# The choice of experts spread over more weight halves, its softmax moved into the expert stage, and the last norm run among the product segments

## The reference

```
sc    = einsum('nhcd,hckd->nhck', q, sub_keys)       # 8 heads, 2 sides, 128 keys
s_top, i_top = top_k(sc, 16)
cand_s = s_top[:,:,0,:,None] + s_top[:,:,1,None,:]   # 16 x 16 sums of a head
best_s, pos = top_k(cand_s, 16)                      # 16 experts of a head
g     = softmax(best_s)
a     = gelu(hc . u[expert]) * g                     # u, v: 16384 x 1024
out   = sum over experts of a * v[expert]
...
h = h + sigmoid(rmsnorm(h) @ w_gate) * e             # last unit of the last layer
return rmsnorm(h, final_norm)
```

## Time and profile before

| | us |
|---|---|
| median of 3 runs (lowest, highest) | 2161.31 (2157.17, 2176.56) |
| the profiled execution, its span | 2159.17, 2157.3 |
| PE, DVE, ACT busy | 1987.1 (92%), 1481.0 (69%), 1207.8 (56%) |
| first expert stage, of it the choice | 380 to 747, 382 to 579 |
| mean granted TensorE clock | 0.957 |

### The profile page before, as it was taken

How to read it: one execution, slowest core, us unless ns; L and a number is a source line. 1 busy time by engine, 2 the same in 40 slices (tenths; PEclk the granted TensorE clock), 3 DMA queues, 4 the chain that set the end, 5 groups by cost and what they waited for, 6 DMA issues and landing times. The chain is left out here.

```text
span 2157.3 us, 43967 instructions
## 1 busy us (share of the span) xinstructions
PE 1987.1 (92%) x15940; PEld 1904.1 (88%) x15940; DVE 1481.0 (69%) x3043; ACT 1207.8 (56%) x2367; POOL 0.2 (0%) x4
## 2 busy tenths in 40 slices
PE   6998888999999898999999896897999988899996
PEld 6887888999999866999999896897999987799996
DVE  5667655999845499666666587764787567468855
ACT  4455654777765588555555557102565553666544
POOL 0000000000000000000000000000000000000000
PEclk9999998999999999999999997986999989899998
DMA  5433334455566500565656461001565533156552
GB/s 188 147 98 108 121 114 127 150 180 177 177 196 192 174 0 0 185 194 193 191 193 192 136 188 57 1 1 34 179 192 177 185 110 102 36 171 195 177 177 68
DMA packets 96223, 295.98 MB, mean 137 GB/s; under 512 B 9315, under 2 KB 25830, under 8 KB 95974
## 3 DMA queue, kind: packets, MB, share of 16 engines
q1 hardware_dynamic: 96102, 294.35, 43.2%
HBM read 293.26 MB, written 1.05 MB: 136 GB/s over the span
## 5 line engine op out<-in xcount | busy, mean ns | idle before, releaser
L423 DVE TENSOR_TENSOR w_low<-ring,w_high 128x512 fp32r<-128x512 f32 x1102 | 747.9, 688 | 385.3 <-ACT w_high L417 378.0
L449 PE MATMUL bank<-a_high,w_high 128*128 128x256 f32 x3256 | 933.1, 287 | 78.7 <-DVE w_low L423 36.8
L450 PE MATMUL bank<-a_low,w_high 128*128 128x256 f32 x3256 | 916.0, 281 | 0.0
L451 PE MATMUL bank<-a_high,w_low 128*128 128x256 f32 x3256 | 915.6, 281 | 0.0
L417 ACT ACTIVATE w_high<-ring 128x512 fp32r<-128x512 f32 x1102 | 676.6, 627 | 394.2 <-PE bank L451 389.9
L449 PEld LDWEIGHTS bank<-a_high,w_high 128*128 128x128 f32 x3256 | 622.5, 191 | 94.8 <-issue 44.8
L450 PEld LDWEIGHTS bank<-a_low,w_high 128*128 128x128 f32 x3256 | 623.8, 192 | 0.7
L451 PEld LDWEIGHTS bank<-a_high,w_low 128*128 128x128 f32 x3256 | 623.9, 192 | 0.0
L449 PE MATMUL bank<-s_high,w_high 128*128 128x256 f32 x1024 | 283.4, 277 | 2.0 <-DVE s_low L2215 2.0
L450 PE MATMUL bank<-s_low,w_high 128*128 128x256 f32 x1024 | 283.4, 277 | 0.0
L451 PE MATMUL bank<-s_high,w_low 128*128 128x256 f32 x1024 | 283.4, 277 | 0.0
(11 more groups left out here) (351 smaller groups left out, 2041.4 us busy)
## 6 DMA issues: line engine op xcount, KB each, us to landing
ring<-in_stream SPq DMA_DIRECT2D x279, 512.0 KB, 3.6
ring<-in_peer_u SPq DMA_DIRECT2D x128, 512.0 KB, 3.5
ring<-in_peer_v SPq DMA_DIRECT2D x128, 512.0 KB, 3.5
ring<-in_stream SPq DMA_DIRECT2D x32, 256.0 KB, 3.2
x<-in_x SPq DMA_DIRECT2D x4, 256.0 KB, 5.5
arena<-in_mem SPq DMA_DIRECT2D x1, 1024.0 KB, 11.8
out<-x SPq DMA_DIRECT2D x4, 256.0 KB, 2.6
consts<-in_consts SPq DMA_DIRECT2D x1, 640.0 KB, 8.6
```

Source lines behind the costliest of these rows:

```text
L423: self.nc.vector.tensor_tensor(self.w_low[:, h % SLOTS, :], self.raw(h), self.w_high[:, h % SLOTS, :].bitcast(F32), ALU.subtract)\
L449: self.nc.tensor.matmul(to, lh, rh, start=start, stop=False, **more)
L450: self.nc.tensor.matmul(to, lh, rl, start=False, stop=False, **more)
L451: return self.nc.tensor.matmul(to, ll, rh, start=False, stop=stop, **more)
```

## The change

Three edits. (1) In the choice, `best` calls `low()` after every second operation instead of every third for the 128-column tiles, and five times in seven operations instead of every second for the 256-column ones. The choice's scratch starts at column block 96 instead of 84, `hit` moves into `hn`, and ScalarE's first loop has 24 turns instead of 20. (2) The softmax leaves its own block: VectorE subtracts the maximum right after the choice, ScalarE does its three copies and the exponential after turn 24, VectorE normalises after its turn 26, TensorE transposes before its last turn into banks 4 and 5, and VectorE copies the turned numbers at its end. (3) `finish` becomes `last_norm`, a segment whose squares and gains are duties with the keys of the additions to x.

```
-        scratch = 84 * T
+        scratch = 96 * T
-        free_from = 80 // RING
+        free_from = 96 // RING
... TensorE
-                with pe.Fori(1, turns) as it:
+                with pe.Fori(1, turns - 1) as it:
                     turn(it)
+                pe.wait_ge(weighed.sem, weighed.at(1))
+                for n in range(3):
+                    for t in range(TT):
+                        at = (n % 2) * T + t * P
+                        ins = nc.tensor.transpose(self.bank[4 + n // 2][:, at:at + P],
+                                                  side[:, n, t, :], self.const("ident"))
+                ins.then_inc(spun.up(), 1)
+                turn(turns - 1)
... ScalarE
                 act.wait_ge(chosen.sem, chosen.at(1))
-                with act.Fori(free_from, turns) as it:
+                turn(free_from)
+                act.wait_ge(shifted.sem, shifted.at(1))
+                nc.scalar.activation(number, side[:, 0:2, :, :], ACT.Copy)
+                nc.scalar.activation(one, self.const("ident"), ACT.Copy)
+                nc.scalar.activation(less, self.const("iota"), ACT.Copy, scale=-1.0)
+                nc.scalar.activation(g, g, ACT.Exp).then_inc(expd.up(), 1)
+                with act.Fori(free_from + 1, turns) as it:
                     turn(it)
... VectorE
-                with dve.Fori(whole, turns) as it:
+                link(nc.vector.tensor_copy(total.unsqueeze(2), g[:, :, 0:1]))
+                nc.vector.tensor_tensor(g, g, ..., ALU.subtract).then_inc(shifted.up(), 1)
+                for it in range(whole, free_from + 3):
+                    for h in range(it * halves, (it + 1) * halves):
+                        self.split_low(dve, first + AHEAD + h)
+                dve.wait_ge(expd.sem, expd.at(1))
+                link(nc.vector.tensor_reduce(total, g, AX, ALU.add))
+                link(nc.vector.reciprocal(total, total))
+                nc.vector.tensor_tensor(g, g, ..., ALU.mult).then_inc(weighed.up(), 1)
+                with dve.Fori(free_from + 3, turns) as it:
                     for h in range(halves):
                         self.split_low(dve, first + AHEAD + h, it, halves)
+                dve.wait_ge(spun.sem, spun.at(1))
+                for n in range(3):
+                    nc.vector.tensor_copy(turned[:, n, :],
+                                          self.bank[4 + n // 2][:, (n % 2) * T:(n % 2 + 1) * T])
... choose_experts
-        hit = self.at(at + 1024 + 8 * T, PH * PK, PK)
+        hit = self.hn[:, :, :].rearrange("p c (n r) -> p (c n) r", r=PK)
-                done[0] += 1
-                if done[0] % every == 0:
+                done[0] += some
+                if done[0] >= of:
+                    done[0] -= of
                     low()
-            best([... for i in range(r, r + 4)], 3)
+            best([... for i in range(r, r + 4)], 1, 2)
-                best([... for i in range(h, h + 4)], 2)
+                best([... for i in range(h, h + 4)], 5, 7)
... last_norm(self, before, name), in place of finish
+        got, keys = before.ready(name)
+        for c in range(0, DC, 2):
+            duties += [(keys[c], 6, "square", c), (keys[c], 7, "gain", c)]
+        duties += [(keys[-1] + 1, 0, "mean", None), (keys[-1] + 1, 1, "scale", None)]
+        def on_act(act, kind, c):
+            if kind == "square":
+                act.wait_ge(*got[c])
+                nc.scalar.activation(hn[:, c:c + 2, :], x[:, c:c + 2, :], ACT.Square)\
+                    .then_inc(squares.up(), 1)
+            elif kind == "gain":
+                if c == DC - 2:
+                    nc.scalar.activation(self.small[:, T:T + 1], self.const("ones")[:, 0:1], ACT.Sqrt)
+                    act.wait_ge(mean.sem, mean.at(1))
+                    nc.scalar.activation(inverse, inverse, ACT.Sqrt).then_inc(root.up(), 1)
+                act.wait_ge(squares.sem, squares.at(c // 2 + 1))
+                for n in range(c, c + 2):
+                    nc.scalar.activation(x[:, n, :], x[:, n, :], ACT.Copy,
+                                         scale=self.param("final_norm_2", n)).then_inc(gained.up(), 1)
... build
-            k.run(k.ffn(1, first, "mla_o"))
-        with k.room(2 * T):
-            k.finish()
+            segments = k.ffn(1, first, "mla_o")
+            k.run([*segments, k.last_norm(segments[-1], "ple_gate.1")])
```

More of the change, by code:

```diff
@@ L1776, in expert_scores @@
         gelued, chosen = self.counter("gelued"), self.counter("choice_made")
+        shifted, expd, weighed, spun = (self.counter(s) for s in
+                                        ("shifted", "dense_expd", "weights_made", "dense_probs_turned"))
+        side, turned, number, one, less = self.choice_views()
+        g = side[:, 2, :, :].rearrange("p t (h k) -> p (t h) k", k=PK)
+        total = self.small[:, 0:16]
         cut = self.counter("input_high"), self.counter("input_low")
@@ L1950, in choose_experts, with choice_views @@
         return made[0]
+    def choice_views(self):
+        side = self.side.rearrange("p (n t s) -> p n t s", n=3, t=TT)
+        number = self.small[:, T:2 * T].bitcast(BF16).rearrange("p (n t s) -> p n t s", n=2, t=TT)
+        one, less = (self.hn[:, 3, n * P:n * P + P // 2].bitcast(BF16) for n in range(2))
+        return side, self.hn[:, 0:3, :], number, one, less
     def expert_weights(self, hot):
         nc = self.nc
-        side = self.side.rearrange("p (n t s) -> p n t s", n=3, t=TT)
@@ L1956, in expert_weights @@
-        turned = self.hn[:, 0:3, :]
-        number = self.small[:, T:2 * T].bitcast(BF16).rearrange("p (n t s) -> p n t s", n=2, t=TT)
-        one, less = (self.hn[:, 3, n * P:n * P + P // 2].bitcast(BF16) for n in range(2))
-        g = side[:, 2, :, :].rearrange("p t (h k) -> p (t h) k", k=PK)
-        total = self.small[:, 0:16]
-        shifted, expd, weighed, spun = (self.counter(s) for s in
-                                        ("shifted", "dense_expd", "weights_made", "dense_probs_turned"))
@@ L2002, in expert_weights @@
+        turned, number, one, less = self.choice_views()[1:]
         apart, left, right, crossed, merged, left_apart, right_apart = (
@@ new lines, in last_norm, with on_sp @@
+        got, keys = before.ready(name)
+        duties = []
+        for c in range(0, DC, 2):
+            duties += [(keys[c], 6, "square", c), (keys[c], 7, "gain", c)]
+        duties += [(keys[-1] + 1, 0, "mean", None), (keys[-1] + 1, 1, "scale", None)]
+        def on_sp(sp):
+            for c in range(0, DC, 2):
+                sp.wait_ge(ready.sem, ready.at(c // 2 + 1))
+                sp.dma_start(self.out[:, c:c + 2, :], x[:, c:c + 2, :]).then_inc(stored.up(16), 16)
+            sp.wait_ge(stored.sem, stored.at(16 * DC // 2))
@@ new lines, in on_pe @@
+        def on_pe(pe):
+            for c in range(DC):
+                pe.wait_ge(squares.sem, squares.at(c // 2 + 1))
+                ins = nc.tensor.matmul(total, self.const("ones"), hn[:, c, :], start=c == 0,
+                                       stop=c == DC - 1)
+            ins.then_inc(sums.up(), 1)
+        def on_act(act, kind, c):
[12 more added lines that the diff above has]
+                                         scale=self.param("final_norm_2", n)).then_inc(gained.up(), 1)
@@ L3056, in _ @@
                                             .broadcast_to([P, 2, T]), ALU.mult).then_inc(ready.up(), 1)
-            @block.sync
-            def _(sp):
-                for c in range(0, DC, 2):
-                    sp.wait_ge(ready.sem, ready.at(c // 2 + 1))
-                    sp.dma_start(self.out[:, c:c + 2, :], x[:, c:c + 2, :]).then_inc(stored.up(16), 16)
-                sp.wait_ge(stored.sem, stored.at(16 * DC // 2))
+        return Segment(duties, on_sp, on_pe, on_act, on_dve, None, None, None)
 def build(nc, dram, out):
```

75 lines of the change are left out of this document (14 added, 61 removed).

## The result

The changed kernel took 2148.95 us (median of 20 runs: 19 of them took 2131.05 to 2165.86, and one 3264.49 at a mean granted clock of 0.555, which the ratio leaves out; without it the median is 2147.52) where the kernel before took 2168.61 beside it; the ratio is 0.9912 [0.9887, 0.9937]. Two further comparisons of the same kernel gave 0.9883 [0.9850, 0.9916] and 0.9939 [0.9909, 0.9969]. The mean of the three, 0.9911, is 19 us. The forecast was 22.8 us or 1.05% (a ratio of 0.9894), with "faster by over 1%" the likeliest; what came is a gain just inside the 1%. Two of the three intervals hold 0.9894, so the times alone hardly tell 19 us from 22.8; the traces do. The profiled execution took 2143.39 us (span 2141.6) where 2137 was forecast.

What follows compares the result with a forecast made beforehand. TensorE, busy nearly all the time, was taken as the bound, with VectorE handing out w_low too late during the choice. 13.8 + 5.0 + 4.0 = 22.8 us off the profiled 2159.2 gave 2136.4, stated as 2137; range 2130 to 2149.

Steps and rivals of the forecast that it cites:

- faster by over 1%: Whole kernel: a gain of more than 1% (21.6 us) in time, given a chance of 0.50.
- part 1: Choice of experts, its w_low calls spread over 180 halves: 17.3 us gained less 3.5 of stalls, net 13.8 us.
- The bound: First expert stage: during the choice VectorE hands out w_low too late, 1.491 us a half against 1.360 after it.
- So the length becomes TensorE's: ... 180 x 1.360 = 244.8: Choice of experts: 180 halves at TensorE's 1.360 us take 244.8 us instead of 262.1, a gain of 17.3 us.
- I take 1.5 us for the first token tile, 2.0 for the second: 3.5 in all: Where ranks become numbers: TensorE stalls for late w_low, 3.5 us in all, bounds none to 4.9 us.
- They are hidden today ... So 0: ScalarE's loop in the first expert stage: table loads, 62 where there were 40, stay hidden and cost 0.
- B: Rival, turns with table loads: the low behind the second load is late, 22 x 0.5 = 11 us, 2148; chance 0.16.
- D: Rival, first w_high of 31 turns: one table load each exposed in full, 40 us, slower at 2176; chance 0.04.
- C: Rival, the choice: ScalarE's loads bound it, not VectorE; 6.3 us lost instead of 17.3 won, 2157; chance 0.08.
- E: Rival, the last norm: it brings nothing, as the late w_high takes it back; 2141; chance 0.05.
- Part 2: Softmax moved inside the first expert stage: 7.1 - 1.5 - 1.6 + 1.0 = 5.0 us gained.
- Part 3: Last norm among ScalarE's duties: 4.0 us gained despite a later last w_high, bounds 0 and 4.1.

Runs made afterwards that it cites:

- the last `w_high` first: The changed kernel with the last norm's squares and gains one key later, so ScalarE makes the last w_high before them; no ratio given, span 2164.0 us.

## Why the prediction missed, step by step

The change gained 8.7 us in part 1 where 13.8 was forecast; parts 2 and 3 came out near their size. The step that failed is the length of the choice once VectorE no longer sets it: the 3.5 us charged to the ranks parts came to 7.8 to 8.3 in every trace of this spacing, the table loads put at 0 being one cause of it, and the pace of 1.360 us a half did not hold in two of the changed kernel's three traces.

**The bound: right.** VectorE handed out `w_low` too late during the choice; with the new spacing TensorE has no idle time over 80 us of it, and turns went from 11.2 to 13.3 us to 10.88 in the first trace.

**"So the length becomes TensorE's: ... 180 x 1.360 = 244.8": right in one trace of three.** TensorE's own length is not one number. 1.360 us a half is 12 x 113.3 ns; the other is 12 x 117.8 = 1.413, so 254.4 us for 180 halves, 9.6 us of the 17.3. Outside the ranks part the first trace, and that of the spacing alone, ran at the first pace (thirteen turns in 141.4 us); the changed kernel's two others ran at the second (147.0 us). Before, this did little harm: the kernel with the softmax alone keeps the old spacing and had more of the slower pace in these thirteen turns (3.0 us for 2.1), and they took 154.4 us in it for 154.1. There VectorE sets the length and a slower TensorE waits less. The change made TensorE the bound of the choice and so exposed it. The slower pace's parts of the stage, 2.4, 9.1 and 12.2 us, are that; the third trace's stage is 2.6 us longer than that of before. Which pace an execution gets is luck as far as the runs show.

**"I take 1.5 us for the first token tile, 2.0 for the second: 3.5 in all": here it failed in every trace.** The waits themselves are 3.7 us in the first trace, as forecast. What they cost is more: in the nine turns from 536 to 642, the ranks parts and what lies between, TensorE is 7.8 us over nine times 10.88, of which the breaks of its stream are 5.4 (the waits and what the matmuls around them start late) and the slower pace 2.3; with the spacing alone it is 8.3. So the term was 4.3 to 4.8 us too small, of the 5.1 that part 1 fell short. The reason was wrong in part as well. VectorE's 26.94 us against 24.5 held 0.82 us of waiting for a late `w_high`; with the loads gone the same operations take 25.8 us, which is still over 24.5, and the waits are zero. So the long average did not bring them.

**"They are hidden today ... So 0" for the table loads: wrong in the ranks part, right elsewhere.** Turns outside it are 10.88 us with both loads in them, which refutes the rivals B and D as they were stated, for every turn; the count of 62 was right. In the ranks part a load and an operation of 2.3 us meet, and the late low behind a load, which is B's mechanism, is at work there: taking the loads away ended all the waits and 4.8 to 5.3 of the 5.4 us of breaks. The slack had been followed in a turn where VectorE's pieces are 0.5 to 0.9 us, and carried over to one where they are not. The Trainium skill (ScalarE: Activation LUTs, What ACT_TABLE_LOAD costs) gives a load of about 1283 ns and a drain to about 2.66 us; the trace agrees with the first (1283 ns, x31) and shows none of the second (548.25 to 549.55).

**C** is refuted by the 708 matmuls. **E** too: the last norm brought its part.

**Part 2: right in size, with some luck.** Boundary and stage behind it 115.0 to 106.6, 8.4 us for 7.1 + 1.0 forecast. The 1.0 was for a clock that stays up, and it does so in seven of the eleven traces with this edit; in the other four the gain is 7.1 to 7.6. The stall behind the exponential was 2.1 us of turn for 1.6, the transposes 0.67 for 1.5. Net 5.6 for 5.0.

**Part 3: near in the trace, 2.5 to 4.0 (3.1 in the mean) for 4.0**, with `w_high` behind four gains, a wait of 5.42 us, and the clock back early enough for the last sums (four in 1.13 us).

**The sum by runs.** Spacing 8.7, softmax 5.6, last norm 3.1 to 4.0: 17 to 18 us, beside 19 us in the times; 22.8 was forecast, and part 1 is the 5 us between. The time itself, 2137 forecast and 2148.95 measured, is off for a second reason: it was counted from the profiled 2159.2 us, and the kernel before had a median of 2168.61 in the 20 runs beside the changed one. In the untouched stretch the changed kernel's traces are 3.3 to 9.5 us longer than before's; part of it is where the granted clock falls in the attention. Forty microseconds of before and of after, each from 110.0 us behind the same `w_low`:

```profile
1419.70:1459.70 40.00, 36.28 (x433) 35.06 (x431) 23.72 (x48) 2.35 (x6) 0.00 (x0) 0.77 0.01 2
```
```profile
1406.40:1446.40 40.00, 36.28 (x346) 35.08 (x345) 19.02 (x38) 2.14 (x5) 0.00 (x0) 0.63 0.01 1
```

433 matmuls started in the one, 346 in the other. The kernel with only the last norm changed shows the long form as well (193.2 us for this piece against 187.6 before), and up to here it is the same program as the one before; two kernels with all three edits have the short form (185.3 and 187.6), and the 14 traces lie between 185.3 and 196.0. So the change is not what brings the long form; as far as these traces show it is chance.

## What to carry to other kernels

When a change makes TensorE the bound of a stretch, cost it at the pace of several executions, not at the best one: what the old bound hid (here 4.5 ns a matmul) comes with the gain. Charge a stall with more than the engine's idle time: here 3.7 us of waits made 5.4 us of breaks. Two small delays that each fit into the slack, a table load and a long operation, can fail together; a slack found in one turn holds only for turns whose longest uninterrupted piece is the same. And where the forecast lies at the border between two answers, as 1.05% did at 1%, neither can be called likely; 0.50 to 0.46 said nearly that. A short fall of the granted clock behind a wait (0.78 over 7.6 us, 1.6 us lost) is easily taken for an effect of the edit: compare the clock of the window before looking for another cause.

## What the runs showed that was not expected

TensorE's 128x256 matmuls have two paces at a granted clock of 1.00 (2.4 GHz): starts 113.3 ns apart or 117.8. A stretch keeps its pace until the next gap in the stream (over 3070 matmuls in the second expert stage) and changes only at one. No length of the gap was found that decides: behind starts of about 140 to 160 ns, of 200 and of 300 ns apart both follow. The listed matmul goes from 276 to 281 ns. Of the weight loads, in the slower pace one of the three passes takes 192 ns and the other two keep their 188; in the usual pace all three take 188. Here the changed kernel's first trace and that with the last `w_high` first, both from 900 to 1000 (groups of weight loads):

```profile
L449 PEld LDWEIGHTS bank<-s_high,w_high 128*128 128x128 f32 x294 | 55.2, 188 | 0.0
```
```profile
L449 PEld LDWEIGHTS bank<-s_high,w_high 128*128 128x128 f32 x284 | 54.5, 192 | 0.0
L450 PEld LDWEIGHTS bank<-s_low,w_high 128*128 128x128 f32 x283 | 53.1, 188 | 0.0
L451 PEld LDWEIGHTS bank<-s_high,w_low 128*128 128x128 f32 x283 | 53.1, 188 | 0.0
```

Which pass it is differs: in six windows at the slower pace it was twice each of L449, L450 and L451. The sum of the slower pace was 13 to 36 us of a trace, in a spread of 2132.4 to 2167.8 us of span. Taken off, the changed kernel's three spans agree, with the luck named above. What sets the pace stays open. The Trainium skill (TensorE: Matmul & The Clock Gate, Wait — 56ns, not 53.3ns?) gives a back-to-back distance of N/2.4 GHz and some 2.5 ns. An estimate from it for 256 columns is 109.2 ns; no run here shows this value, and the measured distances are 4.1 and 8.6 ns above it.

ScalarE's hardware loop, entered with another table than its body leaves, has its loads inside the body: 62 executed loads, 79.6 us of ScalarE, which one dummy gelu ahead of each loop took away, for two loads at the dummies. With the spacing alone the second loop is entered with the gelu table, and there it has none.
